# All low parts of the expert weights on VectorE, none on GpSimd, and the expert outputs evicted by ScalarE

## The reference, cut to what matters

```python
for e in range(N_EXPERTS):
    hid = jax.nn.silu(t @ w1[e]) * (t @ w3[e])
    out = out + gate[:, e:e + 1] * (hid @ w2[e])
```

## Time and profile before

| | |
|---|---|
| median of three executions | 4076.0 us (4073.84 to 4079.07) |
| span of the profiled execution | 4075.8 us |
| expert blocks in that execution: first gate matmul of block 0 to the last down matmul | 3563.4 to 4040.4 us |
| busy in the span: PE, DVE, ACT, POOL | 3430.7, 1700.2, 1158.2, 877.2 us |

### The profile page before, as it was taken

The page is one execution under the profiler, slowest core; times in us unless marked ns, Lnnn a source line. Parts: engine busy times, 40 slices in busy tenths (PEclk is TensorE's granted clock), DMA queues, the critical chain, the costliest instruction groups (busy, mean ns, idle before and its releaser), DMA issues.

```text
span 4075.8 us, 56124 instructions
## 1 busy us (share of the span) xinstructions
PE 3430.7 (84%) x21944; PEld 2234.1 (55%) x21944; DVE 1700.2 (42%) x2418; ACT 1158.2 (28%) x1521; POOL 877.2 (22%) x437
## 2 busy tenths in 40 slices
PE   7999888877848999999999986665777799599996
PEld 5878555533313444687825544444777544277674
DVE  2110345558882000211011013335676410399997
ACT  4431344422221000333110012222222100266663
POOL 4444000000000000344400000001111000189996
PEclk9999999988878999999999985556998799799998
DMA  3323311111201222232372110000000022399996
GB/s 104 94 88 124 139 41 41 41 44 44 59 28 46 74 75 72 77 93 88 93 244 78 58 45 11 10 31 8 4 4 4 2 83 77 119 341 365 355 362 225
DMA packets 106895, 396.78 MB, mean 97 GB/s; under 512 B 11680, under 2 KB 11696, under 8 KB 106240
## 3 DMA queue, kind: packets, MB, share of 16 engines
q1 hardware_dynamic: 95040, 347.42, 25.3%
q0 software_dynamic: 8400, 35.15, 2.3%
q10 hardware_dynamic: 3312, 12.06, 0.7%
HBM read 361.55 MB, written 33.03 MB: 97 GB/s over the span
## 4 chain that ended last, share of the span: by engine, by line
PE 64%; DVE 22%; issue 8%; ACT 2%; DMA 1%; DVEq 1%; POOL 1%; ACTq 0%; SPq 0%; POOLq 0%
PE psum L853 8%; PE psum L196 6%; PE psum L197 6%; PE psum L198 6%; DVE er_r L2249 6%; PE psum L1519 6%; PE psum L488 4%; DVE mem L801 4%; PE psum L1024 4%; PE psum L2064 3%; PE psum L1173 2%; PE psum L496 2%; PE psum L1155 2%; PE psum L938 2%; PE psum L860 1%
## 5 line engine op out<-in xcount | busy, mean ns | idle before, releaser
L186 POOL TENSOR_TENSOR ring_r<-ring,whi 128x1024 fp32r<-128x1024 f32 x132 | 316.0, 2413 | 924.8 <-ACT whi L181 924.8
L2249 POOL TENSOR_TENSOR er_r<-er,eh 128x1024 fp32r<-128x1024 f32 x134 | 426.3, 3218 | 51.1 <-ACT eh L2237 51.1
L2249 DVE TENSOR_TENSOR er_r<-er,eh 128x1024 fp32r<-128x1024 f32 x134 | 368.0, 2785 | 0.0
L1519 PE MATMUL psum<-mem 64*64 64x64 f32 x9664 | 264.3, 234 | 88.1 <-DVE mem L1834 61.0
L1519 PEld LDWEIGHTS psum<-mem 64*64 64x64 f32 x9664 | 249.9, 147 | 102.3 <-DVE mem L1834 69.8
L707 PE MATMUL psum<-xn,ring 128*128 128x512 f32 x512 | 238.0, 628 | 69.2 <-ACT mem L743 64.8
L196 PE MATMUL psum<-ffn_xh,ring_r 128*128 128x512 f32 x704 | 279.6, 397 | 19.3 <-DVE xn_r L209 19.3
L197 PE MATMUL psum<-ffn_xh,whi 128*128 128x512 f32 x704 | 280.7, 399 | 0.0
L198 PE MATMUL psum<-xn_r,whi 128*128 128x512 f32 x704 | 279.0, 396 | 0.0
L2237 ACT ACTIVATE eh<-er 128x1024 fp32r<-128x1024 f32 x268 | 260.7, 1071 | 8.5 <-DMA er<-experts 8.2
L707 PEld LDWEIGHTS psum<-xn,ring 128*128 128x128 f32 x512 | 103.0, 203 | 204.2 <-issue 199.0
(11 more groups left out here) (440 smaller groups left out, 5849.6 us busy)
## 6 DMA issues: line engine op xcount, KB each, us to landing
ring<-stream SPq DMA_DIRECT2D x359, 512.0 KB, 3.6
er<-experts SPq DMA_DIRECT2D x276, 512.0 KB, 5.5
xs_dram<-zero_row POOLq DMA_DIRECT2D x1, 12288.0 KB, 38.4
xs<-xs_dram SPq DMA_DIRECT2D x23, 512.0 KB, 6.1
ys_dram<-y_t ACTq DMA_DIRECT2D x23, 512.0 KB, 5.8
mem<-rpb POOLq DMA_DIRECT2D x8, 512.0 KB, 4.3
resid<-x_t SPq DMA_DIRECT2D x1, 2048.0 KB, 7.7
spill<-resid POOLq DMA_DIRECT2D x1, 2048.0 KB, 6.6
```

Source lines behind the costliest of these rows:

```text
L186: pool.tensor_tensor(ring_r[:, s, :, :], ring[:, s, :, :], f(whi[:, s, :, :]), ALU.subtract).then_inc(w_lo, 1)
L1519: ins = pe.matmul(psum[o, bank, n * L:(n + 1) * L], lhs(n)[r], rhs(n)[r], start=i == 0 if start is None else start, stop=i == len(terms) - ...
L2249: eng.tensor_tensor(er_r[:, at, :], er[:, at, :], f(eh[:, at, :]), ALU.subtract).then_inc(done, 1)
```

## The change

It concerns only the loop over the routed blocks. DVE makes the low parts of all four slabs of a group, in the order 0, 1, 2, 3, and POOL's share with its loop is taken out. PE waits for one semaphore, `e_lo_dve`, with the slab's number. DVE's `take_y` is taken out; ACT reads banks 5 and 6 itself, in `store`, with the same waits that `take_y` had, just ahead of issuing the transfer. Block 0's eight slabs (`lo_first`) stay split between DVE and POOL.

```diff
-        def lo_part(eng, done, kind, b):
-
-            for j in ((0, 2) if done is e_lo_pool else (1, 3)):
+        def lo_part(dve, kind, b):
+
+            for j in range(4):
                 at = SLOT[kind] + j
-                eng.wait_ge(e_hi, slab_number(kind, b, j) + 1)
-                eng.tensor_tensor(er_r[:, at, :], er[:, at, :], f(eh[:, at, :]), ALU.subtract).then_inc(done, 1)
+                dve.wait_ge(e_hi, slab_number(kind, b, j) + 1)
+                dve.tensor_tensor(er_r[:, at, :], er[:, at, :], f(eh[:, at, :]), ALU.subtract).then_inc(e_lo_dve, 1)
...
-            pe.wait_ge(e_lo_dve if j % 2 else e_lo_pool, b * 6 + (2 * kind + j // 2 - 1))
+            pe.wait_ge(e_lo_dve, slab_number(kind, b, j) - 3)
...
-            lo_part(pool, e_lo_pool, 0, 1)
-
-            with pool.Fori(1, LAST) as b:
-                lo_part(pool, e_lo_pool, 1, b)
-                lo_part(pool, e_lo_pool, 2, b)
-                lo_part(pool, e_lo_pool, 0, b + 1)
...
-            def store(b):
+            def store(b, used):
+                act.wait_ge(e_used, used)
+                if not is_block(b, 0):
+                    act.wait_ge(y_st, b * 16)
+                for n in range(2):
+                    act.activation(y_t[:, n * T:(n + 1) * T], psum[:, 5 + n, :], ACT.Copy).then_inc(y_out, 1)
                 act.wait_ge(y_out, b * 2 + 2)
                 act.dma_start(ys_dram[bass.ds(b * P, P), :], y_t[:, :]).then_inc(y_st, 16)
...
-            def take_y(b, used):
-                dve.wait_ge(e_used, used)
-                if not is_block(b, 0):
-                    dve.wait_ge(y_st, b * 16)
-                for n in range(2):
-                    dve.tensor_copy(y_t[:, n * T:(n + 1) * T], psum[:, 5 + n, :]).then_inc(y_out, 1)
...
             def block(b, odd):
-                if not is_block(b, 1):
-                    take_y(b - 2, b * 12 - 4)
-                lo_part(dve, e_lo_dve, 1, b)
+                lo_part(dve, 1, b)
                 gate_up(b)
                 h_low(b - 1)
                 if not is_block(b, LAST):
                     x_low(b + 1, 1 - odd)
-                lo_part(dve, e_lo_dve, 2, b)
+                lo_part(dve, 2, b)
                 hidden(b, b * 12 + 4)
-                lo_part(dve, e_lo_dve, 0, b + 1)
+                lo_part(dve, 0, b + 1)
```

More of the change, by code:

```diff
@@ L2279, in moe_pool @@
                                             xt[:, t, :], None).then_inc(scattered, 16)
-            lo_part(pool, e_lo_pool, 0, 1)
-            with pool.Fori(1, LAST) as b:
-                lo_part(pool, e_lo_pool, 1, b)
-                lo_part(pool, e_lo_pool, 2, b)
-                lo_part(pool, e_lo_pool, 0, b + 1)
-            lo_part(pool, e_lo_pool, 1, LAST)
-            lo_part(pool, e_lo_pool, 2, LAST)
-            lo_part(pool, e_lo_pool, 0, NB)
             pool.wait_ge(y_st, NB * 16)
@@ L2438, in block @@
                 if not is_block(b, 1):
-                    store(b - 2)
+                    store(b - 2, b * 12 - 4)
                 act.wait_ge(e_used, b * 12)
@@ L2454, in moe_act @@
             h_high(LAST)
-            store(LAST - 1)
-            store(LAST)
+            store(LAST - 1, 12 * NB - 4)
+            store(LAST, 12 * NB)
         picked = rt[10]
@@ L2612, in moe_dve @@
             hidden(0, 8)
-            lo_part(dve, e_lo_dve, 0, 1)
+            lo_part(dve, 0, 1)
             def block(b, odd):
-                if not is_block(b, 1):
-                    take_y(b - 2, b * 12 - 4)
-                lo_part(dve, e_lo_dve, 1, b)
+                lo_part(dve, 1, b)
                 gate_up(b)
@@ L2634, in moe_dve @@
             h_low(LAST)
-            take_y(LAST - 1, 12 * NB - 4)
-            take_y(LAST, 12 * NB)
             for t in range(4):
```

## The result

The changed kernel takes 4014.88 us (median of four, 4013.99 to 4015.84) against 4075.82 (median of four, 4073.84 to 4079.07). The ratio is 0.9848, with a 95% interval of 0.9834 to 0.9862: some 61 us faster. The profiled execution has a span of 4012.4 us, 63.4 less than the 4075.8 of before.

What follows compares the result with a forecast made beforehand. PE (17.8 us a block) and transfers (18.0) were taken to bound the changed loop, DVE plus POOL before (20.39). Gains of 48.1 (loop), 7.5 (tail) and 0.3 (last eviction) sum to 56 us off 4075.8: 4020 us, range 4009 to 4043.

Steps and rivals of the forecast that it cites:

- That POOL and DVE take turns at the low part: In the loop the two engines alternate at low parts instead of sharing them: 2378 + 1211 is 3.59 us a pair.
- DVE 16.6 us a block: DVE's load in the changed loop: twelve low parts 13.6 us plus five small operations 3.0, against 20.39 before.
- ACT 15.0: ACT's load a loop block: sigmoid, `hh`, `xbh` 1.92 us, high parts 11.49, copies 1.10, waits and issue some 0.5.
- The order of the lists: One loop block laid out from the end of PE's gate: every slab is 2 us or more early.
- last sign of being wrong: In the loop, a sigmoid starting late after the gate because ACT was behind with copies, making `sig_t` and `xbl` late.
- ACT's waits for landings: In the loop, the last up slab lands at 12.2, ACT reads it at 12.7; landing may grow by some 3 us.
- The period, 18.1 us: Each of 21 loop blocks takes 18.1 us instead of 20.39: slower bound plus 0.1 for seam waits; 48.1 us gained.
- rival A: Transfers bind the loop earlier, at 370 to 385 GB/s: 4041 to 4056 us; sign: ACT idle 1 us a block; chance 0.13.
- The tail, 7.5 us: From block 22's gate through the last down product: 27.1 us becomes 19.6, so 7.5 us less.
- The head, nothing: Before the loop, blocks 0 and 1: block 1's gate ends at 3584.5 us as now (3584.96), no gain, no loss.
- Rival B: Loop transfers are already at their cap (358 GB/s, 20.5 us a block): only the tail gains, 4068 us; chance 0.03.
- Rival C: Loop low parts on DVE stay long without POOL; at 1.7 us each, 55 us more, 4131; chance 0.04.

Runs made afterwards that it cites:

- head start: Changed kernel with DVE's four low parts of block 1's gate moved before block 0's hidden tile; 4012.29 us, ratio 0.9850.
- two products: Changed kernel without the third matmul of each product, 48 matmuls a block instead of 72; 4010.91 us, ratio 0.9832.

## Why the prediction was right

The time was forecast at 4020 us with a range of 4009 to 4043, and is 4014.9.

- **That POOL and DVE take turns at the low part**: right, and shown by the runs in which POOL's part was varied. DVE's low part is 1.22 us throughout and 1.13 from start to start, as read from the four of block 0.
- **DVE 16.6 us a block**: measured 17.73 less 1.00 idle, 16.7. **ACT 15.0**: busy 294.46 of 351 us, 14.9 a block; the two copies were 1.06 us, priced at 1.10.
- **The order of the lists does no harm**: right for these 21 blocks. ACT starts the sigmoid behind PE's gate in the first 15 of 19 blocks; in the last four it stands behind ACT's own copies, 0.6 us each. PE never waits for it. It is the beginning of what the prediction named as its last sign of being wrong, a sigmoid held up by copies, and it comes from ACT's waits for landings.
- **The period, 18.1 us**: the one term of the loop off in size. It was the transfers' 18.0 plus 0.1 for seams; measured was 17.73, which is PE's own term (3 x 5.5 + 1.23 = 17.73; the prediction rounds it up to 17.8). The rate of 408 GB/s was a little low: over 341 to 351 us the runs with queued requests show 411 to 413. And no waits at the seams came on top, since 12 places in the ring let a load take 7.7 us (11.1 at most) without PE noticing. 21 x 0.37 = 7.8 us, which is what the loop gave beyond the 48.1 of the sum (56.0). Part of this is the length of the loop: with the reserve used up, the period is 17.83 (the run with a head start).
- **ACT's waits for landings**: the layout had none, and they are 32.7 us in the 19.8 blocks of the stretch, 1.65 a block. That is over the 1 us a block that the prediction set as the sign of rival A, and the rival's mechanism is indeed there. ACT's idle time took the waits up.
- **The tail, 7.5 us**: measured 7.7. PE stands still for 1.71 us before the last down product, then runs on at a granted clock of 1.00. The profile names DVE's `hl` as the releaser, where I had ACT's copies of block 21. The two end within 0.1 us of each other (`hl` at 3970.72 us, held up until 3970.1 by DVE's last low part; the copies at 3970.81), and PE needs both, so which one decided stays open.
- **The head, nothing**: -0.4, as laid out.
- **Rival A** (transfers bind early) had the right mechanism and the wrong number: they do bind, but at a rate at which PE binds too. **Rival B** (358 GB/s is all there is) is refuted by 412. The 358 of the earlier trace rows were want of requests, since the same loads and stores went faster once PE freed their places sooner. **Rival C** (the low part stays long without POOL) is refuted by 1220 ns with DMA at 412 GB/s beside it.

## What to carry to other kernels

When two engines share a kind of work and both look busy, add the shortest durations that each shows alone. If the sum of both comes near the period, they may be taking turns; a run in which the second engine does the same work for nobody tells whether they do. Then try taking the slower one out altogether, not giving it less: one low part in four on POOL still cost 25 us here. Relieving one of the two of other work was worth nothing meanwhile (ratio 1.0000). Of the three kinds of work tried on POOL beside DVE's low parts, only the memset, which reads nothing from SBUF, was free.

After such a gain, look at what comes next before going on, and whether a margin shrinks from block to block, as ACT's did here, before calling the loop settled. Here PE, transfers and (with the eviction left on it) DVE lay within some 0.1 us of each other at 17.7 to 17.8 us a block, so that a third less work on PE left the period at 17.76.

## What I had not expected of the hardware

A single core moved 411 to 413 GB/s in 512 KB transfers, loads and stores mixed, over 341 to 351 us, in each run whose period was bound by PE or by the transfers. A load's median from issue to landing is 5.4 us in the kernel before, and 7.7, 10.0 and 12.1 us at this rate (the changed kernel, the head start, two products), with no throughput lost.

DVE beside POOL is not stretched in an operation that takes one input from PSUM and one from SBUF: `hid_t` takes 674 ns beside POOL's subtractions and 680 in the changed kernel, where POOL does nothing.
